# Hybrid encoder trunk on one core: the norm of the first RWKV tile's keys, the HGRN state updates and the first RWKV rates change their places

## The reference, cut to what matters

```python
# HGRN2 (4 heads of 128): D = k' v per chunk, S_{t+1} = gam * S_t + D_t
o = inter + intra          # inter = (q*exp(G)) @ S_in, intra = att @ v
o = head_rms_norm(o, norm_g, HG_EPS)
# RWKV-7 (8 heads of 64)
u = u + (token_shift(u) - u) * mu
r, k, v, xw, xa, xg = split_cols(u, RW_SPLITS)
w_log = -softplus(-(w0 + tanh(xw) @ w_up)) - 0.5   # the decay rate
a = sigmoid(a0 + xa @ a_up)                        # the second rate
kk = k * k_k;  kk = kk / max(norm(kk), 1e-12)      # norm of the keys
```

## Time and profile before

| | |
|---|---|
| median of three executions | 3105.27 us (3102.40 to 3106.46) |
| the profiled execution: its own time, and its span | 3102.91 us, 3101.1 us |
| busy in the span: PE, PE weight loads, DVE, ACT, POOL | 2999.5, 2449.0, 1362.0, 635.1, 2344.7 us |
| granted TensorE clock, mean | 0.992 |

### The profile page before, as it was taken

How to read it: one execution, slowest core, us unless ns; L and a number is a source line. 1 busy time by engine, 2 the same in 40 slices (tenths; PEclk the granted TensorE clock), 3 DMA queues, 4 the chain that set the end, 5 groups by cost and what they waited for, 6 DMA issues and landing times.

```text
span 3101.1 us, 47691 instructions
## 1 busy us (share of the span) xinstructions
PE 2999.5 (97%) x20178; PEld 2449.0 (79%) x20178; DVE 1362.0 (44%) x1765; ACT 635.1 (20%) x1031; POOL 2344.7 (76%) x1877
## 2 busy tenths in 40 slices
PE   8999999989999999999899999999999999999996
PEld 7888877777778888888788888777777788888884
DVE  4221233765637462211762213238565555622127
ACT  1000124643310020000310002354432100200021
POOL 8988796742259989988899987867331799898875
PEclk9999999999999999999999999999999999999998
DMA  4332242111113333333233323422110233333322
GB/s 135 101 102 96 89 129 69 51 50 34 30 55 95 122 102 102 96 101 95 89 96 103 100 96 95 121 61 58 37 36 23 69 101 124 100 104 95 96 88 88
DMA packets 201488, 266.60 MB, mean 86 GB/s; under 512 B 12305, under 2 KB 130429, under 8 KB 201277
## 3 DMA queue, kind: packets, MB, share of 16 engines
q1 hardware_dynamic: 194624, 243.51, 25.8%
q10 hardware_dynamic: 6652, 20.05, 1.7%
HBM read 257.22 MB, written 6.29 MB: 85 GB/s over the span
## 4 chain that ended last, share of the span: by engine, by line
PE 83%; POOL 8%; DVE 5%; issue 2%; ACT 1%; DMA 0%; POOLq 0%; SPq 0%; DVEq 0%; ACTq 0%
PE ps L852 70%; POOL w_lo L1178 4%; POOL w_hi L1175 4%; PE ps L404 1%; PE ps L422 1%; PE ps L416 1%; PE ps L1051 1%; PE ps L1029 1%; PE ps L1045 1%; PE ps L1058 1%; PE ps L899 1%; PE ps L1098 1%; PE ps L486 0%; DVE hT_lo L1674 0%; PE ps L381 0%
## 5 line engine op out<-in xcount | busy, mean ns | idle before, releaser
L1175 POOL TENSOR_TENSOR w_hi<-w_raw,zero 128x512 fp32r<-128x512 f32 (+2 forms) x936 | 1085.3, 1159 | 649.9 <-PE ps L852 607.9
L1178 POOL TENSOR_TENSOR w_lo<-w_raw,w_hi 128x512 fp32r<-128x512 f32 (+2 forms) x936 | 1286.6, 1375 | 73.2
L852 PE MATMUL ps<-hT_hi,w_hi 128*128 128x512 f32 (+1 forms) x2368 | 927.7, 392 | 14.1 <-POOL w_lo L1178 11.4
L852 PE MATMUL ps<-hT_hi,w_lo 128*128 128x512 f32 (+1 forms) x2368 | 905.7, 382 | 0.0
L852 PE MATMUL ps<-hT_lo,w_hi 128*128 128x512 f32 (+1 forms) x2368 | 905.5, 382 | 0.0
L852 PEld LDWEIGHTS ps<-hT_hi,w_hi 128*128 128x128 f32 x2368 | 443.9, 187 | 123.8 <-POOL w_lo L1178 21.8
L852 PEld LDWEIGHTS ps<-hT_hi,w_lo 128*128 128x128 f32 x2368 | 443.7, 187 | 89.2
L852 PEld LDWEIGHTS ps<-hT_lo,w_hi 128*128 128x128 f32 x2368 | 444.2, 188 | 84.4 <-issue 2.9
L1746 DVE TENSOR_TENSOR act_raw<-silu,ps 128x512 f32<-128x512 f32 x88 | 59.9, 681 | 616.9 <-PE ps L852 616.9
L852 PE MATMUL ps<-w_hi,aT_hi 128*128 128x512 f32 x704 | 274.6, 390 | 0.0
L852 PE MATMUL ps<-w_lo,aT_hi 128*128 128x512 f32 x704 | 273.9, 389 | 0.0
(11 more groups left out here) (305 smaller groups left out, 3530.5 us busy)
## 6 DMA issues: line engine op xcount, KB each, us to landing
w_raw<-in_w_in SPq DMA_DIRECT2D x104, 512.0 KB, 3.6
w_raw<-in_ffn_wg SPq DMA_DIRECT2D x176, 256.0 KB, 2.8
w_raw<-in_ffn_wu SPq DMA_DIRECT2D x176, 256.0 KB, 3.1
w_raw<-in_ffn_wd SPq DMA_DIRECT2D x88, 512.0 KB, 3.6
w_raw<-in_w_in SPq DMA_DIRECT2D x96, 128.0 KB, 2.3
w_raw<-in_w_out SPq DMA_DIRECT2D x16, 512.0 KB, 3.7
w_raw<-in_ple_gate SPq DMA_DIRECT2D x16, 512.0 KB, 3.7
ln_rows<-in_ln_g ACTq DMA_DIRECT2D x8, 512.0 KB, 3.9
```

Source lines behind the costliest of these rows:

```text
L852: ins = nc.tensor.matmul(o, l_, r_, start=first, stop=last, skip_group_check=into is not None)
L1175: nc.gpsimd.tensor_tensor(w_split[0][:, q, kk, 0:w], w_raw[:, r, kk, 0:w], zero[:, 0:1].to_broadcast([P, w]), ALU.add).then_inc(*step("w_h ...
L1178: nc.gpsimd.tensor_tensor(w_split[1][:, q, kk, 0:w], w_raw[:, r, kk, 0:w], w_split[0][:, q, kk, 0:w].bitcast(F32), ALU.subtract).then_inc( ...
```

## The change

It puts the state updates ahead of all three `lora_mix` on DVE; on PE the rates behind the HGRN output products, with any of the eight banks allowed for them; and 11 and 17 blocks ahead of and behind the sums of squares where 9 and 18 were. On ACT all of tile 0's copies stand ahead of `rates`, `norms_keys` stands right behind `decays`, the three clears come behind it, and the copies of tile 1 come last.

```diff
@@ rates_pe
-                b = take((name, L, ft), (m, L, ft), core_banks_of(ft - 1))
+                b = take((name, L, ft), (m, L, ft), core_banks_of(ft - 1) if ft else range(8))
@@ tensor
                     ins.then_inc(*step("hgd_done", L, t))
-                rates_pe(pe, take, L, 0)
...
                     ins.then_inc(*step("hgo_done", L, t))
-                advance(fill, 9)
+                rates_pe(pe, take, L, 0)
+                advance(fill, 11)
                 key_norms_pe(pe, take, L, 0)
-                advance(fill, 18)
+                advance(fill, 17)
@@ scalar
-            def rkv_inputs(L, ft, ms=range(3)):
-                for m in ms:
+            def rkv_inputs(L, ft):
+                for m in range(3):
...
-                rkv_inputs(L, 0, (0,))
+                rkv_inputs(L, 0)
                 rates(L, 0)
-                rkv_inputs(L, 0, (1, 2))
                 nc.scalar.activation(lora_x[:, 1, :], lora_x[:, 1, :], ACT.Sigmoid).then_inc(*step("lora_act", L, 1))
                 nc.scalar.activation(lora_x[0:32, 2, :], lora_x[0:32, 2, :], ACT.Sigmoid).then_inc(*step("lora_act", L))
-                nc.scalar.activation(bm[:, :, :, 0, :].rearrange("p d t n -> p (d t) n"), all_units(mask64(R64_EYE)), ACT.Copy)
-                nc.scalar.activation(bm[:, :, :, 1, :].rearrange("p d t n -> p (d t) n"),
-                                     zero[:, 0:1].unsqueeze(2).to_broadcast([P, 2 * NT, HEAD]), ACT.Copy)
-                nc.scalar.activation(km[:, :, :, :, :].rearrange("p d t a n -> p (d t a n)"), zero[:, 0:1].to_broadcast([P, 1024]),
-                                     ACT.Copy).then_inc(*step("rw_clear", L))
...
                 norm_squares(L, 0)
                 decays(L, 0)
+                norms_keys(L, 0)
+                nc.scalar.activation(bm[:, :, :, 0, :].rearrange("p d t n -> p (d t) n"), all_units(mask64(R64_EYE)), ACT.Copy)
+                nc.scalar.activation(bm[:, :, :, 1, :].rearrange("p d t n -> p (d t) n"),
+                                     zero[:, 0:1].unsqueeze(2).to_broadcast([P, 2 * NT, HEAD]), ACT.Copy)
+                nc.scalar.activation(km[:, :, :, :, :].rearrange("p d t a n -> p (d t a n)"), zero[:, 0:1].to_broadcast([P, 1024]),
+                                     ACT.Copy).then_inc(*step("rw_clear", L))
                 rkv_inputs(L, 1)
-                norms_keys(L, 0)
@@ vector
-                lora_mix(L, 0)
                 now("hg_glast", L)
                 for t in range(NT - 1):
...
-                lora_mix(L, 1)
-                lora_mix(L, 2)
+                for m in range(3):
+                    lora_mix(L, m)
```

## The result

| | before | changed |
|---|---|---|
| median of four executions each | 3105.2 us (3102.4 to 3106.46) | 3082.51 us (3081.33 to 3082.65) |
| the profiled execution, and its span | 3102.91 us, 3101.1 us | 3082.65 us, 3080.9 us |
| busy PE, DVE, POOL in the span | 2999.5, 1362.0, 2344.7 us | 2993.6, 1374.7, 2349.6 us |
| granted TensorE clock, mean | 0.992 | 0.995 |

The ratio is 0.9927 (95% interval 0.991 to 0.9945): faster by 0.73%, where 0.69% and 3084 us were forecast. The profiled execution of the kernel before is the one that the prediction read; it is none of the four.

A forecast was written before the change was run, and what follows sets the result against it. PE was taken to bound the kernel, busy nearly all the span, so only its waits and slow clock could yield time. Gains of 9.8 and 11.6 us, together 21.4, turned the median 3105.27 into 3084 us; range 3077 to 3096.

The forecast's parts named there:

- First gap and its clock: PE's wait ahead of the rates goes: 2.45 and 2.41 us, plus 1.66 us of slow clock in layer 1.
- The clock term: Layer 1's first 80 output products return from 6.74 to 5.08 us: 1.66 us, bounds 0 and 1.66.
- The chain: Behind the first gap, DVE, ACT and PE times let `pairs` start without a wait; the 5.96 us gap goes in both layers.
- rival 3: ACT table changes cost more than their load when work follows closely: 3094 us; chance 0.01.
- DVE gives `rw_kd` at 655.8 + 3.45 = 659.25: Layer 0 ahead of `pairs`: DVE takes 3.45 us behind `rw_rn`, so `rw_kd` comes at 659.25.
- POOL keeps up even if more DVE work slows it by a third: Weight splits in the 27 blocks: POOL busy 13.56 of 19.50 us, so it keeps up even a third slower.
- The 2.7 us of cover: Ahead of `pairs` in layer 0: `rw_kd` at 659.25, PE arriving at 661.9, so no wait and 2.7 us left.
- 0.2 us of new waits per layer: PE's 25th block waits for ACT's first tile-1 copy, now behind the clears: 0.2 us, bounds nothing and 3.1.
- Clock at the second gap: `pairs` to first `strips` runs at full clock again: 1.6 us gained in layer 0, 1.8 in layer 1.
- The waits inside the core stay as they are: No gain or loss inside the core, since DVE and ACT enter it idle, as before.
- The sum: Layer 0 gains 9.8 us and layer 1 11.6, together 21.4; 3084 us against the median.
- rival 1: Short new PE waits at the third block, sums of squares or 25th block lower the clock: 3090 us; chance 0.14.

The follow-up runs named there:

- wts_early: rates_early with the loads of the small RWKV weights issued one weight slot earlier; 3082.45 us, ratio 0.993.
- before_again: The kernel before the change, word for word, profiled once more; 3108.7 us in a single execution.
- rates_early: Changed kernel with rates back ahead of the HGRN output products, `lora_mix` 0 and ScalarE's first copies in their old places; 3085.15 us, ratio 0.9935.
- pool_hold: Changed kernel with POOL held until DVE is through with line 656 before splitting tile 2's weights from the second slot on; 3079.9 us, ratio 0.9917.
- b9_18: Changed kernel with 9 and 18 blocks around the sums of squares in place of 11 and 17; 3084.2 us, ratio 0.9939.
- hold_again: The pool_hold kernel, unedited, measured once more with more rounds beside the changed kernel; 3079.77 us, ratio 0.9924.

## Why the prediction was right, and where not

**First gap and its clock: right.** 2.45 and 2.41 us are gone and the 80 products take 5.08 us in both layers. The updates were in time. What the gap waited for was left unsaid, though the row called it "issue"; wts_early shows that it was SP's loads. The clock term is no constant: the same gap lowered the clock in layer 1 of before, in both layers of before_again and in neither of rates_early, so 1.66 us is what this execution had to give, not a property of the gap.

**The chain: right up to the norm.** Forecast and measured: sums of squares wanted at 649.3 and 649.66 with their input 0.6 and 0.7 us ahead (648.34 + 0.61 = 648.95), `rw_rn` at 655.8 and 655.97, clears done at 657.8 and 657.96, the copy's bank wanted without a wait of PE: ACT had 0.28 us to spare there, where the forecast had taken 0.2 us of wait. The third block had its bank and no wait. Each change of table cost 1.28 us and no more (652.10 to 653.40), now in work that follows closely: rival 3 is out, and the Trainium skill's drain (ScalarE: Activation LUTs, What ACT_TABLE_LOAD costs) is not seen here either.

**The step that failed is "DVE gives `rw_kd` at 655.8 + 3.45 = 659.25".** It came at 662.36. The 3.45 us were read where POOL was idle (its last split had ended at 665.56); in their new place the five instructions run beside the splits. The trace of the kernel before had the right price in it: line 626 beside a split took 1.29 us, and five of that length would be 6.45 us, an estimate; 6.35 were measured. The step "POOL keeps up even if more DVE work slows it by a third" looked at POOL's side of the collision and not at DVE's. The 2.7 us of cover became 0.17 us of wait, and the two instructions behind, stretched too, made 0.98 us more. Forecast were 0.2 us of new waits per layer, at the 25th block; measured were none there and 1.15 us here. pool_hold shows that without POOL's splits none of it is left.

**Clock at the second gap: right in kind, given back in part.** `pairs` takes 1.10 us for 1.98. From `pairs` to `strips` it is 666.26 - 662.46 = 3.80 us in both layers, for 4.36 and 4.60; without the new wait it is 2.82, so the clock gave 1.54 and 1.78 where 1.6 and 1.8 were taken.

**"The waits inside the core stay as they are": wrong, in favour.** S to X fell by 1.61 and 2.65 us, of which the extra block ahead of S accounts for 0.68. In layer 0 the rest is 0.93 us. The listed waits of PE in this stretch add up to 9.30 us before and 8.64 after, so 0.66 us of it is waits: in the third tile the 0.71 us for `k_tok` is gone and 1.02 for `inv` is 0.79, while others grew, one from 0.97 to 1.39. The last 0.27 us stays open. b9_18 ties the third tile's waits to the count of 28 blocks, since with 27 they return. In layer 1 the clock had fallen behind these waits and no longer does.

**The sum.** Layer 0 was 9.6 for a forecast of 9.8: the core's 0.93 us made up for the new waits. Layer 1 was 12.5 for 11.6, by the clock in the third tile. The 1.67 us lost between the layers is no work of the change: run again, the changed kernel has 1258.68 us there and a span of 3078.9. So that 20.2 us came so close to 21.4 is partly luck: 1.15 us of new waits per layer, where 0.2 was forecast, were made up for by gains in the core that the forecast had put at nothing. No rival came about: the new waits of rival 1 are there, in another place, but the clock stayed at 1.00 through them.

## What to carry over

A duration is good for the place in which it was read: before an instruction is moved, look what the engine that it collides with does at its new place, and price both of the two, not only the one that seems busy. A wait that the profile puts down to "issue" deserves a look at the load queue before engines are reordered; moving a load by one slot gave here what moving the rates gave. And a block moved into a full stretch changes which waits meet later on, by as much as some of the terms one works out: S to X is 1.2 and 2.5 us longer in b9_18 than in the changed kernel, of which the block itself is 0.68.

## What the runs showed of the hardware

**Short gaps lower the clock in some executions and not in others.** A gap of 2.65 us in layer 0 of rates_early left it at 1.00, one of 2.57 us in before_again was followed by 0.58; windows of the two kernels, in this order:

```profile
634.00:636.00 2.00, 2.00 (x34) 1.74 (x34) 1.86 (x3) 1.66 (x3) 2.00 (x2) 1.00 0.55 156
```

```profile
634.00:636.00 2.00, 1.88 (x6) 0.41 (x6) 1.90 (x2) 0.00 (x1) 1.92 (x3) 0.58 0.85 219
```

The clock also fell with no gap over 1.4 us ahead of it: behind three waits of 0.7 to 1.0 us close together (2319 to 2325 us in before, clock 0.50 from 2326), and in hold_again behind waits of 1.38 and 0.32 us in the second tile of layer 1 (0.50 in 2246 to 2248). The changed kernel has these two waits there as well, 1.38 and 0.33 us, at 1.00.

**The same long gap costs more or less, here by where in it the clock falls.** Between the layers PE idles 5.80 us ahead of line 899 in the changed kernel and 5.78 us when run again. The clock is low for about as long in both, but in the one it falls later and stays low until 1540, 6 us into PE's work, and in the other it is back by 1538:

```profile
1532.00:1534.00 2.00, 0.00 (x0) 0.00 (x0) 1.96 (x3) 1.24 (x1) 0.65 (x1) 0.80 0.10 22
...
1538.00:1540.00 2.00, 2.00 (x11) 2.00 (x11) 1.90 (x5) 2.00 (x6) 0.00 (x0) 0.50 0.00 0
```

```profile
1532.00:1534.00 2.00, 0.05 (x1) 0.08 (x2) 1.93 (x4) 1.24 (x1) 0.56 (x1) 0.50 0.16 14
...
1538.00:1540.00 2.00, 2.00 (x19) 2.00 (x19) 1.90 (x5) 2.00 (x6) 0.00 (x0) 1.00 0.00 0
```

The whole stretch from X to K of layer 1 takes 1258.65 to 1258.88 us in six of the fourteen executions of the table and 1260.24 to 1260.51 in the other eight, whatever the kernel. That the place of the fall makes this difference was looked for in these two traces alone.
